# Who multiplies the exponentials of attention: VectorE or GpSimd

## What is computed

```python
m = jnp.maximum(jnp.max(s, axis=-1, keepdims=True), sink)     # attention A, with sinks
e = jnp.exp(s - m)
pr = e / (jnp.sum(e, axis=-1, keepdims=True) + jnp.exp(sink - m))
out = jnp.einsum('bnkgqs,bnskd->bnqkgd', pr.astype(v.dtype), vb)
...
pr = jax.nn.softmax(s, axis=-1)                               # attentions B, C, M, X
return jnp.einsum('bhqk,bkhd->bqhd', pr.astype(v.dtype), v)
```

## Time and profile before

| what | us |
|---|---|
| median of 3 runs | 2173.32 (2171.52 to 2173.62) |
| profiled execution, own time | 2173.41 |
| its span in the trace | 2171.6 |
| TensorE busy | 2105.5 (97%) |
| VectorE busy | 1345.4 (62%) |
| ScalarE busy | 1048.8 (48%) |
| GpSimd busy | 30.7 (1%) |

### The profile page before, as it was taken

One profiled execution on the slowest core, in us unless ns is written; L12 is line 12 of the kernel. 1 busy time (PEld: TensorE's weight loads), 2 busy tenths in 40 slices (PEclk: granted clock), 3 DMA queues, 4 the chain that ended last, 5 costly groups with the idle time before them and its releaser, 6 DMA issues.

```text
span 2171.6 us, 25749 instructions
## 1 busy us (share of the span) xinstructions
PE 2105.5 (97%) x10458; PEld 1753.9 (81%) x10458; DVE 1345.4 (62%) x1789; ACT 1048.8 (48%) x1249; POOL 30.7 (1%) x41
## 2 busy tenths in 40 slices
PE   7999799999999999999999999999999999999997
PEld 6888678888788888888878787888888888888886
DVE  4545765546554565554675655799888746666664
ACT  5444654445444454544557445546545544444442
POOL 1000000000100000000100000000000000000000
PEclk9999999999999998999999999999999999999999
DMA  7554315554555441555544444477699988776762
GB/s 254 185 194 174 136 61 199 191 194 155 196 193 191 163 151 59 190 183 194 199 175 146 146 174 151 165 235 237 232 281 270 284 316 312 271 263 257 272 260 83
DMA packets 95300, 433.72 MB, mean 200 GB/s; under 512 B 7536, under 2 KB 40448, under 8 KB 50384
## 3 DMA queue, kind: packets, MB, share of 16 engines
q1 hardware_dynamic: 93856, 426.50, 56.0%
q0 software_dynamic: 1328, 5.58, 0.7%
HBM read 397.45 MB, written 34.60 MB: 199 GB/s over the span
## 4 chain that ended last, share of the span: by engine, by line
PE 74%; issue 18%; DVE 5%; ACT 3%; DMA 1%; POOL 0%; DVEq 0%; POOLq 0%; SPq 0%; ACTq 0%
PE bank L255 22%; PE bank L257 22%; PE bank L256 22%; PE bank L260 3%; PE bank L1891 2%; DVE w_lo L245 2%; PE bank L720 1%; PE bank L742 1%; ACT w_hi L240 1%; ACT x_hi L282 1%; ACT gated L309 0%; DVE stat L788 0%; DMA parked_a<-one_i 0%; PE bank L1724 0%; DVE arena L813 0%
## 5 line engine op out<-in xcount | busy, mean ns | idle before, releaser
L245 DVE TENSOR_TENSOR w_lo<-raw,w_hi 128x2048 fp32r<-128x2048 f32 x340 | 778.0, 2290 | 546.6 <-ACT w_hi L240 546.5
L240 ACT ACTIVATE w_hi<-raw 128x2048 fp32r<-128x2048 f32 x340 | 650.7, 1915 | 762.1 <-PE bank L257 742.4
L255 PE MATMUL bank<-w_hi,x_hi 128*128 128x512 f32 (+1 forms) x2092 | 827.1, 395 | 20.4 <-DVE w_lo L245 6.4
L257 PE MATMUL bank<-w_hi,x_lo 128*128 128x512 f32 (+1 forms) x2092 | 815.7, 390 | 0.0
L256 PE MATMUL bank<-w_lo,x_hi 128*128 128x512 f32 (+1 forms) x2092 | 815.1, 390 | 0.0
L255 PEld LDWEIGHTS bank<-w_hi,x_hi 128*128 128x128 f32 x2092 | 394.5, 189 | 101.6 <-issue 8.4
L257 PEld LDWEIGHTS bank<-w_hi,x_lo 128*128 128x128 f32 x2092 | 394.2, 188 | 82.4
L256 PEld LDWEIGHTS bank<-w_lo,x_hi 128*128 128x128 f32 x2092 | 394.8, 189 | 76.9
L255 PE MATMUL bank<-w_hi,a_hi 128*128 128x512 f32 x624 | 246.5, 395 | 6.7 <-DVE a_lo L294 3.5
L257 PE MATMUL bank<-w_hi,a_lo 128*128 128x512 f32 x624 | 244.1, 391 | 0.0
L256 PE MATMUL bank<-w_lo,a_hi 128*128 128x512 f32 x624 | 243.9, 391 | 0.0
(11 more groups left out here) (177 smaller groups left out, 1196.1 us busy)
## 6 DMA issues: line engine op xcount, KB each, us to landing
raw<-in_w SPq DMA_DIRECT2D x340, 1024.0 KB, 4.8
parked_t<-arena SPq DMA_DIRECT2D x32, 512.0 KB, 8.8
arena<-parked_t SPq DMA_DIRECT2D x8, 2048.0 KB, 9.5
arena<-parked_a SPq DMA_DIRECT2D x32, 512.0 KB, 5.9
parked_a<-one_i SPq DMA_DIRECT2D x21, 512.0 KB, 7.4
parked_a<-mid SPq DMA_DIRECT2D x11, 512.0 KB, 7.4
h<-in_x SPq DMA_DIRECT2D x2, 512.0 KB, 5.4
one_i<-in_alibi POOLq DMA_DIRECT2D x1, 1024.0 KB, 5.3
```

Source lines behind the costliest of these rows:

```text
L240: act.activation(w_hi[:, u % RING, :, :], raw[:, u % RING, :, :], ACT.Copy).then_inc(*act_done.mark("w_hi", u))
L245: e.tensor_tensor(w_lo[:, u % RING, :, :], raw[:, u % RING, :, :], f32(w_hi[:, u % RING, :, :]), ALU.subtract).then_inc(*dve_done.mark("w_ ...
L255: pe.matmul(out, hi, w_hi[:, s, b, 0:width], start=start, stop=False)
L257: return pe.matmul(out, lo, w_hi[:, s, b, 0:width], start=False, stop=stop)
```

## The change

GpSimd gets a part in each step. The two `tensor_scalar` instructions of every step leave VectorE's list and stand, same operands, same shapes, in GpSimd's, which waits for VectorE's inverse (counter `dve_done`); TensorE's transposes wait for `pool_done` in place of `dve_done`. In all, 88 instructions are moved, 2 x 44: 40 of 128x128 and 48 of 128x256.

```diff
-                    pe.wait_ge(*dve_done["scaled", key, r])
+                    pe.wait_ge(*pool_done["scaled", key, r])
...
-                if self.at(s - 1):
-                    r, m = s - 1, len(self.keys(self.steps[s - 1][0])) * P
-                    dve.wait_ge(*dve_done["inverse", key, r])
-                    for j in range(2):
-                        cols = self.ex[:, r % 3, j * m:(j + 1) * m]
-                        last = dve.tensor_scalar(cols, cols, self.col(4, r)[:, j:j + 1], None, ALU.mult)
-                    last.then_inc(*dve_done.mark("scaled", key, r))
...
+            def pool_step(self, pool, s):
+                r, key, m = s, self.key, len(self.keys(self.steps[s][0])) * P
+                pool.wait_ge(*dve_done["inverse", key, r])
+                for j in range(2):
+                    cols = self.ex[:, r % 3, j * m:(j + 1) * m]
+                    last = pool.tensor_scalar(cols, cols, self.col(4, r)[:, j:j + 1], None, ALU.mult)
+                last.then_inc(*pool_done.mark("scaled", key, r))
+
+        def pool_attend(pool, att):
+            for s in range(len(att.steps)):
+                att.pool_step(pool, s)
```

More of the change, by code:

```diff
@@ L1579, in pool_moba @@
             pool_root(pool, "mix2", 0)
+            pool_attend(pool, att_m)
             pool.wait_ge(*dve_done["o_lo", "M", 7])
@@ L2196, in pool_program @@
             pool_root(pool, "ckv", 16)
+            pool_attend(pool, att_a)
+            pool_attend(pool, att_b)
             pool_root(pool, "ffb0", 0)
@@ L2201, in pool_program @@
             pool_root(pool, "mix1", 0)
+            pool_attend(pool, att_c[0])
+            pool_attend(pool, att_c[1])
             pool_root(pool, "ffb1", 0)
@@ L2205, in pool_program @@
             pool_root(pool, "xa", 0)
+            pool_attend(pool, att_x)
             pool_peer(pool)
```

## The result

The changed kernel takes 2187.47 us (median of 6 runs, 2186.82 to 2189.49) against 2172.2 for the kernel before (6 runs). The ratio is 1.0078 with a 95% interval of 1.0067 to 1.0088. It is slower, as forecast, and inside the range, but by 15.3 us (medians; 16.9 by the ratio) where 6.2 were forecast. The profiled execution took 2189.49 us, 16.1 more than that of before, and so did its span: 2187.7 against 2171.6.

The account below looks back on a forecast made before the run. In the thin attention steps VectorE bounds by little, and GpSimd's slower scaling lengthens the chain: A 0.98, B 1.93, C0 1.02, C1 1.00, X 1.26, M 0, together +6.2 on 2173.4, 2179.6 us; range 2172.5 to 2189.

Parts of the forecast that it names:

- What bounds the steps: Thin attention steps: VectorE bounds B's steps by little; engines hand over small pieces; TensorE's waits for the scaling sum to 7.5 us.
- What GpSimd needs: GpSimd's two scalings per step: estimated 1.0 us a pair at 128 columns and 1.2 at 256, from memset and power rows.
- The bounds themselves: One GpSimd scaling at 128 and 256 columns: from below 0.23 and 0.34 us, from above 0.90 and 1.12.
- a chance of 0.46: Chance of the forecast branch: GpSimd pairs from 0.87/1.07 to 1.4/1.7 us, a loss of +4.4 to +13 us.
- The walk: Attention steps timed instruction by instruction, each starting when its engine is free and its waits have ended; forecast sum +6.2 us.
- the one that had 0.09: The branch of a dear GpSimd, chance 0.09: upper bound +22.2 us, 2195.6; pairs of 1.5 and 1.8 give +15.
- The hand-over of 0.09: From VectorE's inverse to GpSimd's scaling start: 0.09 us, where VectorE's own second instruction waited 0.04.
- M and early C0 at 0: Attention M and C0 before its last two steps: no loss, since a unit of weights covers the scaling with 4.7 us slack.
- Rival 1: GpSimd scaling cheap, pairs 0.46 and 0.66 us: -0.3 us, 2173.1; chance 0.35 within 0.2%, 0.03 for faster.
- Rival 2: GpSimd scaling dear, at the upper bound of its length: +22.2 us, 2195.6; chance 0.09.
- Rival 3: TensorE's low clock level lasting to the end of B, the like in A, C1 and X: 2186.5 us; chance 0.07.
- The lock: In A, VectorE's two-column instructions with two SBUF inputs excluded by GpSimd: some 0.3 us each, sum about 7 us.

Follow-up runs that it names:

- Half the columns: Changed kernel with each GpSimd scaling taking only the first half of its columns, the rest left undivided: 2177.55 us, ratio 1.0026.
- twice the work: Changed kernel with GpSimd executing each scaling twice, first into a tile nobody reads: 2230.11 us, ratio 1.027.
- B alone: Kernel before with only attention B scaled by GpSimd, the other five by VectorE: 2178.16 us, ratio 1.0032.
- the two kernels with fillers: Identity transposes added on TensorE only where it waits: changed kernel 2183.13 us, ratio 1.0063; kernel before 2164.07 us, ratio 0.9978.
- two experiments: Changed kernel with VectorE scaling head 0 and GpSimd head 1: 2173.26 us; changed kernel with each GpSimd scaling executed twice: 2230.11 us.

## Why the prediction was off, by its own steps

1. **What bounds the steps: right.** The chain through A, B, late C0, C1 and X is the loop inverse, scaling, transposes, scores, maximum. VectorE has gaps of up to 2.3 us in B now, TensorE's waits for the scaling went from 7.5 us to 18.1 (those of its weight loads from 5.1 to 7.3), and with the clock at 1.00 VectorE's freed time paid for the later scaling only in A.
2. **What GpSimd needs: this is the step that failed.** "With one stream at 0.83 ns: 0.51 and 0.61, a pair 1.0 and 1.2 us". Measured 0.60 and 0.92, a pair of 1.18 and 1.82. The fixed part was taken too high (0.40; it is 0.28) and the rate three times too low (0.83; it is 2.49 ns a column). At 128 columns the two errors nearly cancel, at 256 they don't, and 24 of the 44 steps have 256, among them all that the tails consist of. The bounds themselves, 0.90 and 1.12 at the upper end, held, but by the fixed part alone: the rate in them, 1.66, was too low as well. A memset has no operand to read and a power of two columns has no length, so no row of before held the rate of a multiplication. The right reading of such rows is a wider range between the ends, not a middle with a chance of 0.46. The walk's +13.7 for the measured pair lies above the +13 where that branch ends, in the one that had 0.09.
3. **The walk: right, with the clock given.** With the measured pair it gives +13.7 where it had +6.2 with the assumed one, so 2187.1 us. The measured 2187.47 is so near by luck as well: the profiled execution is at 2189.49, with 4.6 us more than the walk in the four stages and 2.3 less in M and ahead of A. Half the columns, which made the pair nearly the assumed one, cost +5.6. The walk does not foresee where the clock falls: it had +46 where twice the work made +57, and +3.5 where B alone made +7.8 in its trace. The hand-over of 0.09 was 0.10.
4. **M and early C0 at 0: right.** M is 105.54 with GpSimd and 105.53 with VectorE.
5. **Rival 1** (cheap) fell: 1.18 and 1.82 are above its limit of 0.87 and 1.07. **Rival 2** (dear) was at its near end, "pairs of 1.5 and 1.8 give +15". **Rival 3** (clock) was not a rival but came on top: the low stretches in A, B, C1 and X got longer, and the sum had nothing for that. The 4.6 us of point 3 are what they can have cost in the profiled execution; the two kernels with fillers put it at 2.4 or somewhat more. How much it is in the mean of executions stays open. Its argument against, "the new steps are no thinner" than late A with 2.86 of 4 us busy, fell with the pair: in the window of B in which the clock fell (282 to 286) TensorE was busy 2.03 of 4 us, and later it waits 1.41 us in one step. The prediction had named both as signs of being wrong, a pair far from 1.0 and 1.2 and another PEclk in these windows.
6. **The lock** showed in none of A's two-column instructions (147 to 161 ns, before 147 to 162). Seven of them overlap a scaling in the changed kernel, six by their last 25 ns and one (line 794) by its first 77, and none took longer. The engines do hold each other up, as two experiments showed, but not for a whole instruction: the loss was 0.10 to 0.30 us, and it appeared only where the second instruction began less than 0.1 us behind the first.

The Trainium skill, GPSIMD Engine Reference, has one-input operations at roughly line rate (section 4.1) and two-input ones at some 2.6 cycles an element (section 3.1). Here the one-input multiplication by a scalar of the partition takes 2.49 ns, which at that page's 1.2 GHz is an estimated 3.0 cycles, and the two-input product 1.67 ns, an estimated 2.0. The measurement decides: for these forms the order is the other way round.

## What to carry to other kernels

Before work is moved to another engine, find a row of that engine with the same form and two lengths; where there is none, the range must be that of the ignorance. An instruction's price belongs to its form: the same product cost GpSimd 1.82 us as two multiplications by a scalar and 1.04 as one product of tensors. Where TensorE waits in thin steps, its clock may fall, and then a wait can cost more than its own length, as in B alone (+7.8 us where the walk at the clock of before had +3.5); work that it can do in the wait, and only there, is worth a try before anything is moved between the other engines.

## What the runs showed of the hardware

- GpSimd, fp32, 128 partitions: `tensor_scalar` with a scalar per partition 445, 603 and 922 ns at 64, 128 and 256 columns (0.28 us + 2.49 ns a column); `tensor_tensor` with a repeated second input 614 and 1041 ns at 256 and 512 (0.19 us + 1.67 ns a column). VectorE's `tensor_scalar` 284 and 350 ns at 128 and 256.
- GpSimd and VectorE hold each other up: GpSimd's scaling lost 95 and 162 ns to a VectorE scaling that began 0.06 us earlier, and VectorE's split of 128x2048 lost 0.30 us to a GpSimd scaling that began 0.02 to 0.03 us earlier. In both cases the other kept its time to some 5 ns. Where the second began 0.3 us or more behind the first, it lost nothing (a split 2.30 us, eight two-column instructions 148 to 161 ns).
- TensorE's granted clock went to 0.50 in B, with B alone on GpSimd, three times, and in the same stage with fillers in TensorE's waits it stayed at 1.00. The stage then took 22.1 us in place of 27.4.
